# Scaling the attention probabilities on ScalarE in place of VectorE, in a decoder layer with attention, convolutions and a grouped mixture of experts

## What is computed

```python
c = jnp.cumsum(jax.nn.log_sigmoid(f_logit), axis=1)
for i in range(S // Q_BLOCK):                       # 8 blocks of 128 queries
    s = jnp.einsum("bhqd,bhkd->bhqk", qb, kb) * scale
    s = s + c[:, :, lo:hi, None] - c[:, :, None, :hi]
    s = jnp.where(mask, s, -jnp.inf)                # causal
    p = jax.nn.softmax(s, axis=-1)
    outs.append(jnp.einsum("bhqk,bhkd->bhqd", p, vb))
```

## Time and profile before

| what | value |
|---|---|
| three executions | 1652.94, 1654.74, 1655.31 us |
| median | 1654.74 us |
| span of the profiled execution, first to last instruction | 1652.4 us |
| mean granted TensorE clock | 0.988 |
| DMA, mean over the span | 199 GB/s |
| instructions | 20311 |

### The profile page before, as it was taken

One profiled execution on the slowest core, in us unless ns is written; L12 is line 12 of the kernel. 1 busy time (PEld: TensorE's weight loads), 2 busy tenths in 40 slices (PEclk: granted clock), 3 DMA queues, 4 the chain that ended last, 5 costly groups with the idle time before them and its releaser, 6 DMA issues.

```text
span 1652.4 us, 20311 instructions
## 1 busy us (share of the span) xinstructions
PE 1586.1 (96%) x7739; PEld 1316.3 (80%) x7739; DVE 1177.9 (71%) x1480; ACT 846.0 (51%) x1177; POOL 185.4 (11%) x219
## 2 busy tenths in 40 slices
PE   7999999999999999999999998999999999999981
PEld 6788888888888888888788887788888888887770
DVE  3755868595666665432585677899999999998884
ACT  3113111215556554334231324788888888887773
POOL 0000000202212220000000001011111111111110
PEclk9999999999999999999999999999999999999995
DMA  4243525645332322411454567999999999999966
GB/s 156 51 103 51 127 71 88 80 81 149 89 105 66 107 84 66 147 45 45 160 191 118 166 229 261 358 384 371 361 367 366 354 353 350 354 354 357 355 234 217
DMA packets 159065, 329.30 MB, mean 199 GB/s; under 512 B 17999, under 2 KB 87631, under 8 KB 158970
## 3 DMA queue, kind: packets, MB, share of 16 engines
q1 hardware_dynamic: 142826, 289.70, 53.0%
q0 software_dynamic: 16144, 38.32, 7.8%
HBM read 296.75 MB, written 48.52 MB: 209 GB/s over the span
## 4 chain that ended last, share of the span: by engine, by line
PE 88%; DMA 6%; DVE 4%; issue 1%; ACT 0%; SPq 0%; DVEq 0%; POOLq 0%; ACTq 0%
PE ps L767 53%; PE ps L1107 26%; DMA e_raw<-in_w_down 3%; PE ps L882 2%; PE ps L867 2%; DVE e_lo L1976 2%; DMA e_raw<-in_w_up 2%; PE ps L1114 1%; DMA x_raw<-in_x 1%; PE ps L1047 1%; PE ps L1122 1%; DVE zout L2039 1%; DVE zout L2032 1%; DMA z_d<-ye,row_i 0%; PE ps L1014 0%
## 5 line engine op out<-in xcount | busy, mean ns | idle before, releaser
L1976 DVE TENSOR_TENSOR e_lo<-e_raw,e_hi 128x1024 fp32r<-128x1024 f32 x376 | 435.7, 1221 | 24.5 <-ACT e_hi L1433 20.3
L1433 ACT ACTIVATE e_hi<-e_raw 128x1024 fp32r<-128x1024 f32 x376 | 367.6, 1050 | 22.3 <-DMA e_raw<-in_w_down 15.9
L767 PE MATMUL ps<-xt_hi,w_hi 128*128 128x512 f32 x896 | 302.2, 394 | 1.8 <-DVE xt_lo L1539 1.8
L767 PE MATMUL ps<-xt_lo,w_hi 128*128 128x512 f32 x896 | 298.1, 390 | 0.0
L767 PE MATMUL ps<-xt_hi,w_lo 128*128 128x512 f32 x896 | 298.1, 390 | 0.0
L767 PEld LDWEIGHTS ps<-xt_hi,w_lo 128*128 128x128 f32 x896 | 168.1, 188 | 35.7
L767 PEld LDWEIGHTS ps<-xt_hi,w_hi 128*128 128x128 f32 x896 | 167.8, 188 | 34.7 <-ACT xt_hi L1194 2.0
L767 PEld LDWEIGHTS ps<-xt_lo,w_hi 128*128 128x128 f32 x896 | 168.4, 188 | 33.2 <-DVE xt_lo L1539 0.4
L1572 DVE TENSOR_TENSOR w_lo<-w_raw,w_hi 128x512 fp32r<-128x512 f32 x136 | 95.0, 703 | 135.6 <-ACT w_hi L1190 132.3
L1190 ACT ACTIVATE w_hi<-w_raw 128x512 fp32r<-128x512 f32 x136 | 83.8, 628 | 208.0 <-PE ps L767 190.7
L1107 PE MATMUL ps<-e_hi,xe_hi 128*128 128x512 f32 x512 | 163.0, 400 | 7.6 <-DVE e_lo L1976 7.6
(11 more groups left out here) (307 smaller groups left out, 2252.8 us busy)
## 6 DMA issues: line engine op xcount, KB each, us to landing
e_raw<-in_w_up SPq DMA_DIRECT2D x128, 1024.0 KB, 21.8
e_raw<-in_w_down SPq DMA_DIRECT2D x64, 1024.0 KB, 21.7
w_raw<-in_w_in SPq DMA_DIRECT2D x64, 256.0 KB, 4.8
w_raw<-in_w_gate SPq DMA_DIRECT2D x48, 256.0 KB, 3.5
gates_d<-gate_t POOLq DMA_DIRECT2D x16, 512.0 KB, 3.3
gate_s<-gates_d SPq DMA_DIRECT2D x16, 512.0 KB, 3.6
qkv_d<-qkv POOLq DMA_DIRECT2D x12, 512.0 KB, 3.6
w_raw<-in_w_branch SPq DMA_DIRECT2D x24, 256.0 KB, 3.7
```

What stands on the lines that cost most here:

```text
L767: last = nc.tensor.matmul(o(h, c1 - c0), st(k), mv(k, c0, c1), start=start and k == nk[0] and n == 0, stop=h in stop and k == nk[-1] and n ...
L1433: nc.scalar.activation(e_hi[:, (UPT + s) % RSPL, :], e_raw[r][:, s % 2, :], ACT.Copy).then_inc(e_h, 1)
L1976: nc.vector.tensor_tensor(e_lo[:, sp_, :], e_raw[raw_slot(b, s)][:, s % 2, :], e_hi[:, sp_, :], ALU.subtract).then_inc(e_all, 1)
```

## The change

The multiplication of the probabilities by the reciprocal moves from DVE to ACT. ACT waits for the reciprocal (inv_ok) right behind the exponential and its sum, and multiplies in place by a copy with a per-partition scale. DVE keeps the reciprocal and drops its own wait for it. PE's waits are as before.

```diff
--- before.py
+++ after.py
@@ -1248,6 +1248,11 @@
                 nc.scalar.activation(prob[n % 2][:, 0:cut], s_bank(n)[:, 0:cut], ACT.Exp,
                                      bias=rmax[:, n % 2:n % 2 + 1], accum_out=rsum[:, n % 2:n % 2 + 1]).then_inc(exp_ok, 1)
 
+            def normalize(n):
+                act.wait_ge(inv_ok, n + 1)
+                cut = prob[n % 2][:, 0:ntiles(ORDER[n % TT]) * P]
+                nc.scalar.activation(cut, cut, ACT.Copy, scale=rinv[:, n % 2:n % 2 + 1]).then_inc(norm_ok, 1)
+
             def split_pt(n):
                 r = ORDER[n % TT]
                 act.wait_ge(t_ok, n + 1)
@@ -1291,6 +1296,7 @@
                     split_pt(n - 2)
                 if n < STEPS:
                     exponential(n)
+                    normalize(n)
                 if n >= 3 and (n - 3) % TT in PAIRED:
                     output(n - 3)
                 if n < STEPS and g in (1, 3):
@@ -1624,9 +1630,6 @@
 
                 dve.wait_ge(exp_ok, n + 1)
                 nc.vector.reciprocal(rinv[:, n % 2:n % 2 + 1], rsum[:, n % 2:n % 2 + 1]).then_inc(inv_ok, 1)
-                dve.wait_ge(inv_ok, n + 1)
-                cut = prob[n % 2][:, 0:ntiles(ORDER[n % TT]) * P]
-                nc.vector.tensor_scalar(cut, cut, rinv[:, n % 2:n % 2 + 1], None, ALU.mult).then_inc(norm_ok, 1)
 
             def split_pt(n):
                 r = ORDER[n % TT]
```

## The result

| | kernel before | changed kernel |
|---|---|---|
| median of 18 executions | 1655.32 us | 1658.89 us |
| ratio, 95% interval | | 1.0019 (1.0012 to 1.0026) |
| span of the profiled execution | 1652.4 us | 1655.7 us |

Two of the 18 executions of the changed kernel were in a slow state, 7100 and 6074 us, and the ratio leaves them out (the other 16 have a median of 1658.51). By the ratio the change costs 3.1 us, between 2.0 and 4.3. A second set of 12 executions gave 1.0019 again (1.0009 to 1.0029). Both intervals exclude 1, so a slowdown of this size can be told from none, though it lies just under the 0.2% (3.3 us) that the prediction gave as the least; the forecast was 1.8 us.

What follows compares the result with a forecast made beforehand. PE, busy throughout 380 to 660 us, was taken to bound the kernel. Stalls of 0.85 + 0.65 + 0.3 = 1.8 us on the median 1654.74 us gave 1656.5 us, forecast as no change; range 1653.5 to 1659.7 us.

Steps and rivals of the forecast that it cites:

- PE bounds, and DVE's relief is worth nothing: Attention stage: PE busy 280.00 of 280.00 us, so taking 64 multiplications, 41.7 us, off DVE gains nothing.
- The price of the new instruction: ACT's scaling: 297 ns + 0.83 ns a column, 95 ns of it for the per-partition operand; 49.6 us more on ACT.
- The wait for the reciprocal: ACT waits for DVE's reciprocal behind each exponential: about 0.35 us a step, 22 us over 64 steps.
- The chain through DVE's maximum in head 0, steps 0 and 1: Late weights' split delays DVE's next maximum, then V's low part; PE stalls about 0.85 us before step 2's transposes.
- Head 0, steps 2 to 4: Scalings push the tanh, step 3's exponential and V's split; PE's transposes wait about 0.65 us for V's low part.
- Heads 2, 4 and 6: Steps 2 to 4: V's low part ends at 467.22 against PE's 467.13; 0.1 us each, 0.3 us for three heads.
- Nothing at all: Rival: the pipeline swallows the stalls, 1654.7 us; 24 in 100, same verdict as the forecast.
- The signs: Between 380 and 660 us: ACT busy up about 50 us, DVE down 42, PE gaps at V's split.
- A later stage of another length: Sign against the forecast: stages behind attention should only shift by 2 us and otherwise stay as they are.
- slower: Rival: V's low part holds up PE, each link 0.5 us dearer, five places 1.0 us later; 1661.5 us; 13 in 100.
- A table reload: Rival: a copy behind an exponential reloads ACT's tables, 1.28 us each, two a step, 164 us: 1819 us; 1 in 100.
- Faster: Rival: relieved DVE makes V's low part earlier for PE in four even heads, 0.6 us: 1654.2 us; 2 in 100.

Runs made afterwards that it cites:

- changed, again: The changed kernel profiled once more with no edit; ratio 1.0019 (1.0009 to 1.0029), PE's attention stretch 283.59 us.
- V's split first: Changed kernel with V's split ahead of the scaling on ACT in steps 1 and 3 of even heads; PE's attention stretch 281.19 us, +0.27 against before.
- the other four: Changed kernel with scaling last, in odd heads only, or twice; kernel before with ACT only waiting for the reciprocal; PE's attention stretches 280.84, 280.93, 299.95, 281.43 us.

## Why the prediction was right, and where its sum was off

- **PE bounds, and DVE's relief is worth nothing: right.** 41 us less on DVE bought nothing; the kernel with the scaling last is the clean case, at 0.9996.
- **The price of the new instruction: right.** Forecast 1.15, 1.04, 0.51 and 0.40 us for 1024, 896, 256 and 128 columns, measured 1.151, 1.046, 0.509 and 0.402. The 95 ns for a per-partition operand, taken from exponential against copy, hold.
- **The wait for the reciprocal:** 17.6 us against 22.
- **The chain through DVE's maximum in head 0, steps 0 and 1: right.** Forecast 0.85 us (its times give 387.79 - 386.98 = 0.81), measured 0.93; the part through the weights' split was shown alone, 0.31 us.
- **Head 0, steps 2 to 4: right.** Forecast 0.65 us (395.65 - 395.04 = 0.61), measured 0.69; V's low part was forecast at 394.97 and started at 394.93.
- **Heads 2, 4 and 6: this is the term that was mis-sized.** "0.1 us each, 0.3 us for three heads" was 0.35 each, 1.05. I compared the end of V's low part with the old start of PE's transposes and left out the hand-over from DVE to PE, 0.15 us in all the timelines above (386.85 to 387.00, 468.02 to 468.17). It is missing in all five places; in the two large ones it was partly made up by rounding up and by links that came out shorter. The chain on ACT was also a little longer than worked out: on the changed kernel's own clock, which PE's stalls had put 0.74 us behind, the output half starts at 463.42 where I had 463.30, V's high part at 466.72 where I had 466.65, and V's low part ends at 468.02 where I had 467.96. That makes 0.09 + 0.15 + 0.06 = 0.30 us at the place itself; the last 0.05 are lost in the step behind.
- **Sum:** 1.8 us forecast, 2.71 us in the stretch. The median's ratio gives 3.1 us (2.0 to 4.3), which holds the 2.71. What lies between isn't told apart: the stages before and behind attention vary more than that from trace to trace. The size of the forecast was off by a third of what was measured, and its verdict, no change that a measurement can tell, holds only by the 0.2% that it set itself: both intervals exclude 1. "Nothing at all", 1654.7 us, is out.
- **The signs:** ACT's busy time between 380 and 660 us rose by 43 us, not 50. "A later stage of another length", which was to show the forecast wrong, was seen (1.5 us in the first trace, 2.1 in the second) and is no sign of it, since traces that share these stages differ by up to 4.4 us there.
- **The rival "slower"** had the right place; its condition, each link 0.5 us dearer, didn't hold. The rule against multiplication on ScalarE (page "ScalarE: Activation LUTs" of the Trainium skill, Rules for kernel authors) is borne out in its sign for this change and not for this kernel: with the same work on ScalarE in another place nothing was lost. **A table reload** didn't happen: one load. **Faster** didn't either; the 0.14 us by which V's low part led PE in head 0 was the hand-over, and not slack.

The kernel with the scaling last equals the one before; no version beat it, and with PE full in this stage I expect none that only moves work among the other engines to.

## What to carry to other kernels

When an instruction moves to an engine with spare time, its busy time says little; write down what is queued behind it on that engine until the next thing the bounding engine waits for, include the detour by another engine's queue (here weights' split, low part, maximum), and add a hand-over at every change of engine, the last one too. If the moved work has a late reader, as here two steps later, issue it last in the step: that made a change that cost 2.7 us cost nothing and cut the wait for its operand from 17.6 us to 2.1. To judge effects of this size, align two traces at an event of the stage and compare distances; the totals of single executions vary by more.

## What the runs showed of the hardware that I had not expected

- VectorE's scaling of 256 columns took three times as long as that of 384 columns. Groups by form of the kernel before, DVE, and under them GpSimd's split of k:

```profile
L1629 DVE TENSOR_SCALAR prob<-prob,rinv 128x384 f32<-128x384 f32 x8 | 3.4, 421 | 0.3
...
L1629 DVE TENSOR_SCALAR prob<-prob,rinv 128x256 f32<-128x256 f32 x8 | 11.2, 1403 | 0.3
```

```profile
L607 POOL TENSOR_TENSOR k_two<-k_raw,k_two 64x1024 fp32r<-64x1024 f32 x7 | 16.8, 2398 | 22.1 <-ACT k_two L1219 22.1
```

  The 1.84 us of the earlier trace rows is the longest of them. Seven of the eight start while GpSimd splits k (in head 0 from 391.75 to 394.14 us) and take 1.50 to 1.84 us, each ending about 0.15 us behind that instruction. In the last head there is no next k to split, and the eighth took 0.35 us:

```profile
644.61 0.35 DVE L1629 TENSOR_SCALAR prob<-prob,rinv 128x256 f32<-128x256 f32 x1
```

  With the scaling gone from VectorE the GpSimd instruction still takes 2388 ns in place of 2398, so only VectorE lost by it. The page "SBUF — State Buffer" of the Trainium skill (SBUF: two separate sides) has GpSimd and a VectorE instruction in a two-port mode take turns on a shared pair of ports, the later one blocked for the whole of the other; these starts and ends agree with that.
- The stages outside attention differ by up to 0.9 us ahead of it (378.9 to 379.8) and 4.4 us behind it (991.7 to 996.1) between traces of kernels that have the same instructions there. Part of what lies behind goes with TensorE's granted clock. From the transposes of the last attention step, a copy in the output projection (x1t, at 927.99 us in the kernel before) follows after 267.26 to 267.29 us in all ten traces. A pair of weight copies early in the expert stage (e_hi, at 1068.69 us in the kernel before, 1073.21 in the changed one) doesn't:

| granted clock, 1000 to 1070 us | traces | from those transposes to that pair of copies, us |
|---|---|---|
| 1.00 | changed, again; DVE in steps 0 to 3 of even heads | 407.0, 407.2 |
| 0.98 | before; ACT in head 0, step 0 only | 408.0, 408.0 |
| 0.95 | V's split first | 409.7 |
| 0.88 | changed; the other four | 410.6 to 411.2 |

  (The kernel that scales twice reaches attention's end 18 us later and has 0.88 from 1018 to 1088 us too.) The changed kernel is in the first row and in the last, so the clock differs between executions of one and the same kernel. From those copies to the end the traces differ by 4.3 us once more (582.5 to 586.7), and there the order is not that of the clock; what makes them do so stays open.
